# Rows added by GpSimd ahead of a norm's sum, moving columns side by side, and squares that no longer wait for a logarithm: a hybrid decoder step on one core

## The reference

```python
def rmsnorm(x, g):
    y = xf * lax.rsqrt(jnp.mean(xf * xf, axis=-1, keepdims=True) + RMS_EPS)
    return (y * g.astype(jnp.float32)).astype(x.dtype)

def trunk(x, S_init, make_ctx, attend):
    for l in range(DEPTH):
        if l == N_A:
            ctx, new_kv = make_ctx(x)          # shared K/V from rmsnorm(x, norm_kv)
        h = rmsnorm(x, norm_mix[l])
        ...                                     # layer 0: gated recurrence; layer 1: sparse attention
        x = x + o
        x = x + sq_relu_mlp(rmsnorm(x, norm_mlp[l]), w_mlp_up[l], w_mlp_down[l])
    return rmsnorm(x, norm_final), ...

def hgrn_lower_bounds(lb_logits):
    cum = jnp.cumsum(jax.nn.softmax(lb_logits.astype(jnp.float32), axis=0), axis=0)
    return cum - cum[:1]

def compress(kv, pe, w1, w2):                   # windows of 32 positions, 16 apart
    ...
    flat = jnp.moveaxis(blocks, 3, 2).reshape(B, n_cmp, G, CMP_LEN * dk)
    return jax.nn.silu(flat @ w1) @ w2
```

## Time and profile before

| what | value |
|---|---|
| median of 3 runs | 2199.69 us (2198.9 to 2202.35) |
| profiled execution, its time | 2196.9 us |
| its span, first to last instruction | 2195.2 us |
| PE busy | 2054.6 us (94%) |
| DVE, ACT, POOL busy | 611.8, 403.9, 315.7 us |
| mean granted clock | 0.962 |

### The profile page before, as it was taken

One profiled execution on the slowest core, in us unless ns is written; L12 is line 12 of the kernel. 1 busy time (PEld: TensorE's weight loads), 2 busy tenths in 40 slices (PEclk: granted clock), 3 DMA queues, 4 the chain that ended last, 5 costly groups with the idle time before them and its releaser, 6 DMA issues.

```text
span 2195.2 us, 28391 instructions
## 1 busy us (share of the span) xinstructions
PE 2054.6 (94%) x11212; PEld 1713.2 (78%) x11212; DVE 611.8 (28%) x1084; ACT 403.9 (18%) x839; POOL 315.7 (14%) x523
## 2 busy tenths in 40 slices
PE   6999998899999999999889999899739999999997
PEld 5888887788888888888766668686417888888886
DVE  3455456211121000010237753344401221110002
ACT  2344443210000000100225433233200100000000
POOL 2233324000000000000036653340000000000000
PEclk9999999899999999999959999999969999999999
DMA  5222232012222222214350009986891122222221
GB/s 135 74 73 61 69 98 70 19 68 77 76 76 76 77 76 76 76 39 175 96 138 2 1 11 228 184 186 207 269 319 58 39 77 76 67 58 70 74 76 39
DMA packets 216473, 206.83 MB, mean 94 GB/s; under 512 B 13857, under 2 KB 170642, under 8 KB 216242
## 3 DMA queue, kind: packets, MB, share of 16 engines
q1 hardware_dynamic: 197938, 188.67, 30.8%
q10 hardware_dynamic: 18432, 16.79, 2.3%
HBM read 195.38 MB, written 18.42 MB: 97 GB/s over the span
## 4 chain that ended last, share of the span: by engine, by line
PE 85%; DVE 3%; ACTq 3%; SPq 2%; issue 2%; DMA 2%; ACT 1%; POOL 1%; DVEq 0%; POOLq 0%
PE ps L828 51%; PE ps L867 10%; PE ps L1046 5%; PE ps L1039 2%; PE ps L907 2%; ACTq L1671 2%; PE ps L817 2%; PE ps L1100 1%; PE ps L882 1%; PE ps L1122 1%; PE ps L1140 1%; ACTq L342 1%; DMA stream<-in_cache_nsa_kv 1%; PE ps L1248 1%; PE ps L933 1%
## 5 line engine op out<-in xcount | busy, mean ns | idle before, releaser
L828 PE MATMUL ps<-h,stream 128*128 128x260 f32 x2688 | 592.7, 384 | 1.7 <-DVE h L2260 1.7
L828 PEld LDWEIGHTS ps<-h,stream 128*128 128x128 f32 x2688 | 512.3, 191 | 81.5 <-DVE h L2260 2.1
L828 PE MATMUL ps<-big,stream 128*128 128x260 f32 (+1 forms) x2464 | 542.9, 383 | 4.6 <-DVE big L1937 3.9
L828 PEld LDWEIGHTS ps<-big,stream 128*128 128x128 f32 (+1 forms) x2464 | 466.8, 190 | 80.4 <-issue 5.1
L867 PE MATMUL ps<-h,stream 128*128 128x260 f32 x1024 | 236.8, 386 | 5.1 <-DVE h L1792 5.1
L867 PEld LDWEIGHTS ps<-h,stream 128*128 128x128 f32 x1024 | 191.6, 192 | 37.2 <-issue 10.0
L1411 ACT ACTIVATE scratch<-x 128x520 f32<-128x520 f32 x32 | 20.4, 637 | 1052.6 <-DVE x L1925 1052.6
L1925 DVE TENSOR_TENSOR x<-x,ps 128x520 f32 x32 | 22.3, 696 | 537.7 <-PE ps L828 522.1
L1934 DVE SCALAR_TENSOR_TENSOR scratch<-ps,rstd 128x520 f32<-128x520 f32 x64 | 44.8, 700 | 343.2 <-PE ps L828 343.2
L1046 PE MATMUL ps<-big 128*128 128x256 f32 x384 | 99.7, 383 | 0.0
L2106 DVE COPY big<-ps 128x512 f32<-128x512 f32 x80 | 55.3, 691 | 101.1 <-PE ps L1039 78.3
(11 more groups left out here) (308 smaller groups left out, 2032.7 us busy)
## 6 DMA issues: line engine op xcount, KB each, us to landing
stream<-in_w_mlp_up SPq DMA_DIRECT2D x16, 2048.0 KB, 8.3
stream<-in_w_mlp_down SPq DMA_DIRECT2D x16, 2048.0 KB, 8.9
stream<-in_cache_nsa_kv SPq DMA_DIRECT2D x128, 256.0 KB, 6.1
stream<-in_w_hgrn_in SPq DMA_DIRECT2D x32, 512.0 KB, 6.9
stream<-in_cache_nsa_kv SPq DMA_DIRECT2D x128, 128.0 KB
stream<-in_cache_nsa_kv ACTq DMA_DIRECT2D x128, 128.0 KB
stream<-in_cache_win_kv SPq DMA_DIRECT2D x16, 512.0 KB
out<-in_cache_win_kv SPq DMA_DIRECT2D x8, 1022.0 KB
```

Of the source, the lines that this page charges most:

```text
L828: m = nc.tensor.matmul(pair(c)[0:n1, a, :], w[:, k, P * c_local:P * c_local + n1], rhs[:, k, NH * a:NH * a + NH], start=(k == 0), stop=(k ...
```

## The change

There are three edits. First, at four norms POOL adds rows 1 to 6 of the squares to row 0, each when it comes, and PE sums only that row and row 7; at mlp0 the copies to `h` become `early`. Second, the evictions of sample compression write their buffer in the order in which the products read it (`by_parity`), so that a product's 256 columns lie side by side; before, they lay in runs of 8. Third, the first step of the forget bound moves ahead of the copies of `x` on DVE, and its Ln moves behind the squares of mix0 on ACT.

```diff
+        def by_parity(ap):
+            return ap.rearrange("p (a n k) -> p n a k", a=2, k=PAGES // 2)
+
+        def in_rows(ap):
+            return ap.rearrange("p (n a k) -> p n a k", a=2, k=PAGES // 2)
...
+            def squares_added(name):
+                n = turn_of[name]
+                total = squares[:, 0, :]
+                pool.wait_ge(norm["sq"], n * KD + 1)
+                for k in range(1, KD - 1):
+                    pool.wait_ge(norm["sq"], n * KD + k + 1)
+                    m = nc.gpsimd.tensor_tensor(total, total, squares[:, k, :], ALU.add)
+                    if k < KD - 2:
+                        ch.link(m)
+                m.then_inc(norm["added"], 1)
+
+            squares_added("mlp0")
+            squares_added("attn")
             pool.wait_ge(norm["out"], out_count["attn"])
...
+            squares_added("mlp1")
+            squares_added("final")
...
             def norm_sum(name, sq):
                 n = turn_of[name]
-                for k in range(KD):
-                    pe.wait_ge(norm["sq"], n * KD + k + 1)
+                rows = range(KD) if name == "mix0" else (0, KD - 1)
+                for k in rows:
+                    if name == "mix0":
+                        pe.wait_ge(norm["sq"], k + 1)
+                    elif k == 0:
+                        pe.wait_ge(norm["added"], n)
+                    else:
+                        pe.wait_ge(norm["sq"], n * KD + KD)
...
-                rows = TKs[s % 8].rearrange("p (g i a k) -> p g i a k", g=G, a=2, k=PAGES // 2)
-                comp_mul(lambda par: rows[:, :, :, par, :], P, e // 4 % 2, e % 4, 2 + e // 4 % 2).then_inc(sm["mul"], 1)
+                rows = TKs[s % 8].rearrange("p (a n) -> p a n", a=2)
+                comp_mul(lambda par: rows[:, par, :], P, e // 4 % 2, e % 4, 2 + e // 4 % 2).then_inc(sm["mul"], 1)
...
-            act.wait_ge(lb_done, 3)
-            ch.link(nc.scalar.activation(lnb[:, 3, :], lnb[:, 2, :], ACT.Ln))
-            act.sem_inc(lb_done, 1)
+
+            def forget_bound():
+
+                act.wait_ge(lb_done, 3)
+                ch.link(nc.scalar.activation(lnb[:, 3, :], lnb[:, 2, :], ACT.Ln))
+                act.sem_inc(lb_done, 1)
...
-            norm_act("mix0", squares_in, lambda k: act.wait_ge(turn_taken, 3 + k))
+            norm_act("mix0", squares_in, lambda k: act.wait_ge(turn_taken, 3 + k), between=forget_bound)
...
-            norm_act("mlp0", squares, added("out"), late=[(GAIN_MLP, h)])
+            norm_act("mlp0", squares, added("out"), early=[(GAIN_MLP, h)])
...
-                nc.scalar.activation(out, ps[:, TB[s % 3], :], ACT.Copy).then_inc(sm["ev0"], 1)
+                src = ps[:, TB[s % 3], :]
+                if s < WIN:
+                    out, src = by_parity(out), in_rows(src)
+                nc.scalar.activation(out, src, ACT.Copy).then_inc(sm["ev0"], 1)
...
+            dve.wait_ge(turn_taken, 1)
+            z = vec[:, LOGITS:LOGITS + KD]
+            ch.link(nc.vector.tensor_tensor(lnb[:, 0, :], z, z, ALU.subtract))
+            dve.sem_inc(lb_done, 1)
             dve.wait_ge(turned, 2)
```

More of the change, by code:

```diff
@@ L252, in hybrid_step @@
         relu_base = {"up0": 0, "up1": KF}
-        norm = {k: sem("norm_" + k) for k in ("sq", "sum", "sqrt", "out")}
+        norm = {k: sem("norm_" + k) for k in ("sq", "added", "sum", "sqrt", "out")}
         turn_of = {name: n for n, name in enumerate(("mix0", "mlp0", "attn", "mlp1", "final"))}
@@ L1403, in gained, with norm_act @@
                     .then_inc(norm["out"], 1)
-            def norm_act(name, sq, wait_row, early=(), late=()):
+            def norm_act(name, sq, wait_row, early=(), late=(), between=None):
                 n = turn_of[name]
@@ L1416, in norm_act @@
                         gained(gain, out, k)
+                if between:
+                    between()
                 act.wait_ge(norm["sum"], n + 1)
@@ L1768, in _ @@
                 nc.vector.tensor_copy(x[:, k, 0:T], ps[:, k % 4, :]).then_inc(turn_taken, 1)
[L1770 to L1773, removed]
             dve.wait_ge(lb_done, 2)
@@ L2105, in evac @@
                     dve.wait_ge(sm["mul"], m - 7)
-                nc.vector.tensor_copy(out, ps[:, TB[s % 3], :]).then_inc(sm["ev1"], 1)
+                src = ps[:, TB[s % 3], :]
+                if s < WIN:
+                    out, src = by_parity(out), in_rows(src)
+                nc.vector.tensor_copy(out, src).then_inc(sm["ev1"], 1)
             def half_a(n):
```

## The result

The changed kernel takes 2182.23 us in the median of three runs (2181.59 to 2185.44), the kernel before 2199.69: 17.5 us faster in the medians. The ratio as measured is 0.9929 [0.9915, 0.9942], which is 15.6 us; the quotient of these two medians would be 0.9921. The forecast was 2180, its range 2175 to 2187. The profiled execution took 2185.44 us (span 2183.7), 11.5 less than that of before: this pair shows less than the medians do.

A forecast was written before the change was run, and what follows sets the result against it. PE's own work was taken as the bound, with 85% of the span. Terms -4.5 x 3 + 1.0 - 6.0 - 1.2 = -19.7 took the median 2199.69 to 2180.0 us; forecast's own range 2177 to 2184, wider range 2175 to 2187.

The forecast's parts named there:

- mlp0, attn, final: Norm sums at these three places: PE keeps 4 products of 16, 2.50 us against 7.01, -4.5 each.
- mix0: Norm sum at the start: ends at 24.4 us instead of 30.41, so -6.0; bounds -4.0 and -7.9.
- mlp1: Norm ahead of up1: starts 0.5 us earlier, 4 us idle costs 1.5 (bounds 0 and 1.9), net +1.0.
- either passage from up to down: The two gaps between up and down stages: either can gain or lose 1.9 us; not in the sum.
- Columns: Sample compression: products from `scratch` as fast as from other buffers, -1.2 us; bounds 0 and -1.3.
- 1: Clock falls back in the 0.7 us gaps (mlp0, attn) and in mix0's sum: 2186 us; chance 0.15.
- 2: Time won before the sample caches is given back at their loads: 2195 us is left; chance 0.06.
- 3: Scattered writes double both evictions in sample compression: +32 us, so 2212; chance 0.04.
- 4: Steps hold, both up-to-down gaps keep full clock, restart at 29.5 at its better bound: -23.5, 2176 us; chance 0.10.

The follow-up runs named there:

- mlp0_late: The changed kernel with the copies to `h` at mlp0 late again, as before the change; 2187.87 us, ratio 0.9960.
- pool_only: The kernel before with only the first edit: POOL's adds at four norms and early copies at mlp0; 2188.67 us, ratio 0.9960.
- no_columns: The changed kernel without its second edit, so columns in runs of 8 again; 2182.47 us, ratio 0.9923.
- mlp1_eight: The changed kernel with all 16 products of mlp1's sum back on PE and no POOL sum there; 2177.52 us, ratio 0.9904.
- columns_only: The kernel before with only the second edit, the columns side by side in sample compression; 2197.19 us, ratio 0.9995.
- changed_again: The changed kernel itself, unaltered, measured once more; 2185.09 us, ratio 0.9941.
- start_only: The kernel before with only the third edit, the forget bound's steps moved at the start; 2191.28 us, ratio 0.9972.
- early_warm: The changed kernel with mlp1's copies early into free stream slots and unread products behind mix0's sum and ahead of both down stages; 2175.41 us, ratio 0.9899.

## Why the prediction was right, point by point

**mlp0, attn, final: right, -4.3 each for -4.5.** Place, order and cover are those of the text. The term was mis-sized by 0.2: PE takes the two products of row 7 in 1.14 us, not in 0.88; nobody was late, it starts 0.70 us after its last work. POOL's add took 1.28 of the 1.3 to 1.8 allowed, and costs nothing because PE asks 4.1 us later.

**mix0: right, -6.0 inside what the profiles show.** The pair of profiles gives -4.9, but layer 0 starts anywhere between 29.11 and 30.58 in the ten profiles with the edit and no help at the start (mean 29.87), and at 35.51, 35.73 and 37.36 in the three without (mean 36.20): -6.3 in the means. At the end of layer 0 the same ten and three profiles have means of 459.85 and 465.00: 5.1 of it is left there, in a stage that takes anything from 428.3 to 432.9 us. The sum did run at its pace (7.03), as the text took; its lower bound, a slow sum, did not come. Ln's second table load was hidden behind the sum. What varies is the end of the transposes ahead of it, where the sum starts: at 18.46 in the profile of after, at 17.49 in that of mlp0_late.

**mlp1: right in kind, the loss too small.** The start came 0.2 earlier instead of 0.5: the copies end 6.46 behind nsa_out, as the text took, but PE starts 0.34 after them. And up1 lost 1.8 where I took 1.5, inside the bounds of 0 and 1.9 here, outside them in pool_only (2.4), mlp0_late (2.2) and no_columns (2.1). Net +1.6 for +1.0. The kernel that has the gap and the one that fills it (226.32 and 224.69) show the cause. The Trainium skill's page "TensorE: Matmul & The Clock Gate" (Part 1: The HAM clock gate, and HAM oscillation) says that idleness brings the low level back and that a group behind a wait starts slow. All six stages behind an open gap of about 4 us in these profiles agree, with 1.7 to 2.8 us lost. Between this page of the Trainium skill and the row of 1944.34 in the earlier trace rows, which spoke against it, the former was the better guide at this place.

**What the sum left out: +1.7 in down1.** The text said that either passage from up to down can gain or lose 1.9, and took it at zero. At down1 it does not look like a coin: the piece is slow in the five profiles whose up1 started slow, and in none of the other five whose gap there is open. At down0 this reading fails: that piece is slow in seven of the same ten, and up0 had started slow in only one of them (mlp0_late). Why a slow start of up1 would reach a gap 226 us later is open, and that it does is not shown. Counted with it, the shorter sum at mlp1 costs 3.3, and mlp1_eight, which takes it back, is the faster kernel (0.9904 against 0.9929).

**Columns: the 8 ns came, and whether the -1.2 "moves along" is not shown.** The products fell from 387 ns to 379, as predicted. At the end the runs can't tell: the columns alone are 0.9995 [0.9986, 1.0004], which fits -1.2 as well as nothing, and without them the change is 0.9923 [0.9909, 0.9936] against 0.9929 and 0.9941 with them. Compression is followed by a stage that waits for loads. Chain and products of columns_only:

```profile
1653.28 58.06 PE ps L847 x256
```
```profile
L1065 PE MATMUL ps<-big x384: 379/379/631, 1310.3 to 1498.4; 128*128 128x256 f32 x192
```

From the first to the last of these products it needs 188.1 us, before 189.2; from there to nsa_out 154.9, before 152.5 (1651.88 - 1499.4). Over all 14 profiles the two stretches together take 343.2 in the mean of the eight with the edit and 342.8 in the six without. They lie anywhere between 340.1 and 346.9 us, and the same kernel took 346.9 as after and 343.7 as changed_again: scatter of this size covers the 4.1 that the profile of after lost there, and any gain of 1.2.

**The rivals.** 1 fell: the clock stayed at 1.00 behind the gaps of 0.7 us, and up0 took 224.47. What the text took there from the Trainium skill's page "TensorE: Matmul & The Clock Gate" (A second HAM failure mode) is not seen in these gaps. 2 fell as stated: pool_only and start_only keep their gain through the cache stage; only the columns' gain, won inside it, is not seen behind it, and is too small to be. 3 fell: DVE's eviction stayed at 691 ns, ACT's grew by 24 ns into `scratch` only, far below the 0.6 us that would decide. 4 needed the full clock at both passages, which the changed kernel did not have.

**The total.** With the measured sizes, and the columns at nothing, the sum is -6.3 - 12.9 + 1.6 + 1.7 + 0 = -15.9, or 2183.8. The medians of the two measurements of the change, 2182.23 and 2185.09, lie on either side of it; by the ratios (0.9929 and 0.9941, -15.6 and -13.0) it is at the fast end. The forecast was 3.8 faster than this sum: 1.7 is down1, 1.2 the columns, 0.6 mlp1 and 0.6 the three norms, with 0.3 more won at mix0. The first median flattered it by 1.6; that part of the agreement is luck.

What stays open: how much of the 3 us by which early_warm ended above what was expected is the low clock at the end of layer 0. It costs 4.1 in the profiled execution, the other executions left no profile, and the cache stage scatters by more than that. Why the clock comes back later there in two profiles of fourteen is open too.

## What to carry to other kernels

Before you shorten PE's work in front of a wait, look at what ends the wait: if it is another engine's work, the shorter sum becomes idle time, which buys nothing and can cost the clock of the stage behind it (here 1.7 to 2.8 us); move that engine's work ahead first. A few unread products are a cheap test of whether idleness is what a slow stage suffers from, and in this kernel also a cure for the gaps they fill; look in the profile for what became slower elsewhere. Do not count on a gain of 1 us inside a stage ahead of one whose length varies by 6 us from profile to profile: here it could be neither shown nor excluded.

## What the runs showed of the hardware

- Open gaps of 1.9 to 2.0 us ahead of the down stages cost 1.7 in 12 of 20 cases and nothing in 8, with the same instructions on both sides; filled, they cost nothing in 8 of 8. Open gaps of about 4 us ahead of an up stage cost 1.7 to 2.8 in 6 of 6. Gaps of 0.7 us never cost anything that a piece shows.
- A loss of clock can move: with 22 unread products behind the sum of mix0, two of four profiles show the low level at the end of layer 0 (granted 0.50 and 0.71 in two pieces, 4.1 us lost) where twelve others had the second of these pieces at full pace.
- At the start the granted clock reads 1.00 in the window of 12.00 to 18.40 above, and yet the 32 transposes in it run slowly: 6.42 us, where behind unread products they took 3.89. So the granted clock read there does not show PE's pace; the time of a known instruction does.
- ACT's eviction of 128x512 into `scratch` has a median of 622 ns in runs of 8 columns, where the kernel before, which wrote in a row, had 598; into `big` (597), and on DVE, the order of writing cost nothing.
